# Small-block row lists loaded with the expert's other lists, and one semaphore for each small-block row buffer

## The reference, cut to what matters

```
eid_s = eid[order]; tok_s = order // TOP_K; gate_s = gates.reshape(n_asg)[order]   # sorted by expert
def expert_block(args):
    xb, e = args
    return (jax.nn.silu(xb @ w_g[e]) * (xb @ w_u[e])) @ w_d[e]
ybuf = lax.map(expert_block, (xbuf.reshape(n_blocks, MOE_BLK, D_MODEL), block_e))
y = ybuf.reshape(n_blocks * MOE_BLK, D_MODEL)[dest] * gate_s[:, None].astype(xt.dtype)
return jax.ops.segment_sum(y, tok_s, num_segments=n_tok)
```

## Time and profile before

| | us |
|---|---|
| median of three timed runs | 2811.11 |
| profiled execution, its own time | 2801.74 |
| its span (first to last instruction) | 2800.1 |
| PE busy | 2565.7 (92%) |
| DVE busy | 1757.6 (63%) |
| ACT busy | 1606.1 (57%) |
| POOL busy | 889.7 (32%) |

### The profile page before, as it was taken

One profiled execution on the slowest core, in us unless ns is written; L12 is line 12 of the kernel. 1 busy time (PEld: TensorE's weight loads), 2 busy tenths in 40 slices (PEclk: granted clock), 3 DMA queues, 4 the chain that ended last, 5 costly groups with the idle time before them and its releaser, 6 DMA issues.

```text
span 2800.1 us, 59777 instructions
## 1 busy us (share of the span) xinstructions
PE 2565.7 (92%) x19448; PEld 1802.4 (64%) x19449; DVE 1757.6 (63%) x3619; ACT 1606.1 (57%) x2613; POOL 889.7 (32%) x915
## 2 busy tenths in 40 slices
PE   5899999999999999993989899889989788889977
PEld 2345555555555555551878788778878677778866
DVE  5677777777777777776545466456646344446533
ACT  7665555555655555563646477557747445557642
POOL 1132232322322332222333344334434323324422
PEclk9899999999999999997999999999999889999988
DMA  9376666666666666667756677567767445657732
GB/s 317 73 166 164 164 153 158 157 157 154 158 164 163 154 157 157 158 149 227 226 177 181 199 257 256 160 191 255 256 203 257 149 140 164 199 187 255 251 86 46
DMA packets 551307, 507.25 MB, mean 181 GB/s; under 512 B 413803, under 2 KB 413964, under 8 KB 550236
## 3 DMA queue, kind: packets, MB, share of 16 engines
q1 hardware_dynamic: 517372, 405.56, 50.2%
q0 software_dynamic: 33744, 100.60, 14.1%
q10 hardware_dynamic: 144, 0.52, 0.0%
HBM read 322.09 MB, written 87.36 MB: 146 GB/s over the span
## 4 chain that ended last, share of the span: by engine, by line
PE 61%; DMA 21%; issue 8%; POOL 3%; DVE 3%; POOLq 2%; ACT 2%; SPq 1%; DVEq 0%; ACTq 0%
PE psG L611 11%; DMA out_rows<-y,scatter_rows 7%; PE psE L611 6%; PE psF L611 6%; PE psD L611 5%; PE psC L611 5%; PE psG L1929 5%; PE psH L1929 4%; DMA tail_more<-slot_table 4%; DMA xg_more<-hn_rows,tail_more 3%; PE psA L1891 3%; PE psB L1891 3%; PE psH L611 3%; PE psC L1891 3%; PE psD L1891 3%
## 5 line engine op out<-in xcount | busy, mean ns | idle before, releaser
L611 PE MATMUL psG<-wi_all,both_xT 128*128 128x512 f16 x1536 | 346.0, 381 | 4.4 <-DVE qsq L1402 4.4
L611 PEld LDWEIGHTS psG<-wi_all,both_xT 128*128 128x128 f16 x1536 | 148.6, 98 | 181.3 <-issue 9.9
L2022 ACT ACTIVATE unread<-wi_all 128x4096 fp8e4<-128x4096 f32 x62 | 223.7, 3607 | 0.0
L872 ACT ACTIVATE prob<-prob,soft,s_stat 128x256 f32<-128x256 f32 x256 | 150.9, 591 | 99.5 <-DVE soft L1295 99.5
L1828 POOL DMA_INDIRECT out_rows<-y,scatter_rows x79 | 166.4, 2107 | 77.0 <-POOL scatter_rows L1825 68.0
L611 PE MATMUL psE<-wo_all,both_mT 128*128 128x512 f16 x768 | 177.8, 381 | 3.0 <-DMA both_mT<-prob 2.9
L611 PE MATMUL psF<-wo_all,both_mT 128*128 128x512 f16 x768 | 176.2, 379 | 0.0
L2155 DVE SCALAR_TENSOR_TENSOR gate_lo<-wi_all,own,gate_hi 128x2048 f16<-128x2048 f32 x64 | 150.2, 2349 | 38.6 <-ACT gate_hi L2026 38.6
L611 PE MATMUL psC<-wi_all,both_xT 128*128 128x512 f16 x768 | 171.0, 379 | 0.0
L611 PE MATMUL psD<-wi_all,both_xT 128*128 128x512 f16 x768 | 171.0, 379 | 0.0
L2155 DVE SCALAR_TENSOR_TENSOR up_lo<-wi_all,own,up_hi 128x2048 f16<-128x2048 f32 x64 | 147.7, 2349 | 35.2 <-issue 33.2
(11 more groups left out here) (405 smaller groups left out, 7330.5 us busy)
## 6 DMA issues: line engine op xcount, KB each, us to landing
wi_all<-in_w_gate SPq DMA_DIRECT2D x32, 2048.0 KB
wi_all<-in_w_up SPq DMA_DIRECT2D x32, 2048.0 KB, 12.6
wi_all<-in_w_down SPq DMA_DIRECT2D x32, 2048.0 KB
um<-u_rows SPq DMA_DIRECT2D x64, 256.0 KB, 2.7
out_rows<-h SPq DMA_DIRECT2D x32, 512.0 KB, 3.0
xt<-in_x SPq DMA_DIRECT2D x31, 512.0 KB, 3.8
xres<-in_x SPq DMA_DIRECT2D x31, 512.0 KB, 4.6
hn_rows<-xres SPq DMA_DIRECT2D x31, 512.0 KB, 2.9
```

The source lines that it names most:

```text
L611: m = nc.tensor.matmul(ps, left[:, l, k, :], weights.half(r, k, n, width), start=(k == opens and j == 0), stop=(k == closes and j == 2))
L872: s.activation(prob[:, hd, :], prob[:, hd, :], ACT.Exp, bias=ntop[:, hd:hd + 1], scale=inv_s, accum_out=psum_[:, hd:hd + 1]).then_inc(p_sb ...
L2022: s_.activation(unread[:].bitcast(mybir.dt.float8e4), w, ACT.Abs, accum_out=sums(p, n), saturate=False).then_inc(summed, 1)
```

## The change

The lists of the first two small blocks of an expert are now loaded together with its other list, three experts ahead, into `tail_lists`. `big` on GpSimd makes three small copies from it (to `tail_now`, `more` and `first_rows`) and then gathers `xg_more`, issues the list loads for expert e+3, waits for TensorE's transposes of `xg_first`, and gathers the next expert's `xg_first`. The semaphore `tail_rows_in` is split into `first_in` and `more_in`. At the start GpSimd waits for the clearing before it loads any list. The counts of `pending_s` change with the number of copies. The loop over small blocks still reloads `more` and gathers again.

```
-        return 2 * e + 2 * t + 1
-    def more_of(e, t):
-        return 2 * e + t + (1 if is_last(e) else 2)
+        return 4 * e + 2 * t + 2
...
-        def load_list(e):
+        def load_lists(e):
             pool.dma_start(lists[:, bass.ds(e, 1)].rearrange("p o j w -> p (o j) w"),
                            table[bass.ds(e * CAP, BIG), :].rearrange("(j p) w -> p j w", p=P)).then_inc(listed_in, 16)
+            pool.dma_start(tail_lists[0:TAIL, bass.ds(e, 1)].rearrange("p o j w -> p (o j) w"),
+                           table[bass.ds(e * CAP + BIG, 2 * TAIL), :].rearrange("(j p) w -> p j w", p=TAIL)).then_inc(listed_in, 16)
...
-            pool.wait_ge(listed_in, 48 if isinstance(e, int) and e < 3 else 16 * (e + 1))
+            pool.wait_ge(listed_in, 96 if isinstance(e, int) and e < 3 else 32 * (e + 1))
...
+        def tail_of(e, i):
+            return tail_lists[:, bass.ds(e, 1), i].rearrange("p o w -> p (o w)")
+
+        def gather_tail(rows, listing, signal):
+
             pool.indirect_dma_start(rows[0:TAIL, :], None, hn_dram, bass.IndirectOffsetOnAxis(ap=listing[0:TAIL, 0:1], axis=0),
-                                    bounds_check=SEQ + P - 1).then_inc(tail_rows_in, 16)
+                                    bounds_check=SEQ + P - 1).then_inc(signal, 16)
...
         def big(e, p, r, t, ahead):
-            keep_list(first, listed(e, t) + 1)
-            list_tail(more, e, 1, 2 * e + t + 1)
-            gather_tail(xg_more, more, 2 * e + t + 1, None if is_zero(e) else turned(e, t) - 4)
             if ahead:
-                list_tail(first, e + 1, 0, 2 * e + t + 2)
-                gather_tail(xg_first, first, 2 * e + t + 2, turned(e, t) + 1)
+                pool.wait_ge(listed_in, 32 * E if ahead == 1 else 32 * (e + 3))
+            pool.wait_ge(first_in, 16 * (e + 1))
+            if not is_zero(e):
+                pool.wait_ge(more_in, 16 * (e + t))
+                pool.wait_ge(xT_ps, turned(e, t) - 4)
+            hold(pool, held)
+            g.tensor_copy(tail_now[:], tail_of(e, 0)).then_inc(pending_s, 1)
+            g.tensor_copy(more[:], tail_of(e, 1)).then_inc(pending_s, 1)
+            g.tensor_copy(first_rows[:], tail_of(e + 1 if ahead else e, 0)).then_inc(pending_s, 1)
+            pool.wait_ge(pending_s, listed(e, t) + 3)
+            hold(pool, held)
+            gather_tail(xg_more, more, more_in)
             if ahead > 2:
-                load_list(e + 3)
+                load_lists(e + 3)
+            if ahead:
+                pool.wait_ge(xT_ps, turned(e, t) + 1)
+                hold(pool, held)
+                gather_tail(xg_first, first_rows, first_in)
...
         mixed(pool)
+        pool.wait_ge(cleared, 5)
         for e in range(3):
-            load_list(e)
+            load_lists(e)
         for j in range(2):
             gather(0, j)
-        pool.wait_ge(cleared, 7)
...
-        def turn_tail(rows, number):
-
-            pe.wait_ge(tail_rows_in, 16 * number)
+        def turn_tail(rows, landed, number):
+
+            pe.wait_ge(landed, 16 * number)
...
-            turn_tail(xg_first, 2 * e + t + 1)
+            turn_tail(xg_first, first_in, e + 1)
...
-            turn_tail(xg_more, more_of(e, t) + 1)
+            turn_tail(xg_more, more_in, e + t + 1)
...
-            copy_y(2 * e + t, 0, listed(e, t))
+            copy_y(2 * e + t, 0, listed(e, t) + 2)
...
-        for listing in (first, more):
-            v.memset(listing[:], 0).then_inc(cleared, 1)
-        dve.wait_ge(cleared, 3)
-        for listing in (first, more):
-            v.tensor_copy(listing[:, 0:1], cst[:, C_JUNK:C_JUNK + 1]).then_inc(cleared, 1)
+        v.memset(tail_lists[:], 0).then_inc(cleared, 1)
+        dve.wait_ge(cleared, 2)
+        v.tensor_copy(tail_lists[:].rearrange("p e j w -> p (e j) w")[:, :, 0],
+                      cst[:, C_JUNK:C_JUNK + 1].to_broadcast([P, 2 * E])).then_inc(cleared, 1)
```

More of the change, by code:

```diff
@@ L1662, in experts @@
     aT_hi, aT_lo = sb("aT_hi", [P, KE, BIG], F32R), sb("aT_lo", [P, KE, BIG], F32R)
-    lists = sb("lists", [P, E, 2, 2], I32)
-    first, more, tail_now = (sb(f"tail_{w}", [P, 2], I32) for w in ("first", "more", "now"))
+    lists, tail_lists = sb("lists", [P, E, 2, 2], I32), sb("tail_lists", [P, E, 2, 2], I32)
+    first_rows, more, tail_now = sb("first_rows", [P, 2], I32), sb("tail_more", [P, 2], I32), sb("tail_now", [P, 2], I32)
     pending = sb("pending", [P, 2, 2], I32)
@@ L1696, in experts @@
     chosen, named, pending_s = sem("chosen"), sem("named"), sem("pending_s")
-    rows_in, tail_rows_in, added = sem("rows_in"), sem("tail_rows_in"), sem("added")
+    rows_in, first_in, more_in, added = sem("rows_in"), sem("first_in"), sem("more_in"), sem("added")
     xT_ps, xT_hi, xT_lo = sem("xT_ps"), sem("xT_hi"), sem("xT_lo")
@@ L1795, in gather @@
                                     bounds_check=SEQ + P - 1).then_inc(rows_in, 16)
[L1797 to L1809, removed]
-            pool.indirect_dma_start(rows[0:TAIL, :], None, hn_dram, bass.IndirectOffsetOnAxis(ap=listing[0:TAIL, 0:1], axis=0),
-                                    bounds_check=SEQ + P - 1).then_inc(tail_rows_in, 16)
[L1813 to L1817, removed]
+        def tail_of(e, i):
+            return tail_lists[:, bass.ds(e, 1), i].rearrange("p o w -> p (o w)")
+        def gather_tail(rows, listing, signal):
+            pool.indirect_dma_start(rows[0:TAIL, :], None, hn_dram, bass.IndirectOffsetOnAxis(ap=listing[0:TAIL, 0:1], axis=0),
+                                    bounds_check=SEQ + P - 1).then_inc(signal, 16)
         def scatter(d, s):
@@ L1850, in tail @@
             g.tensor_copy(pending[:, 0, :], tail_now[:]).then_inc(pending_s, 1)
-            pool.wait_ge(pending_s, listed(e, t) + 2)
+            pool.wait_ge(pending_s, listed(e, t) + 4)
             hold(pool, held)
-            keep_list(more, listed(e, t) + 3)
-            list_tail(more, e, i + 2, more_of(e, t) + 1)
-            gather_tail(xg_more, more, more_of(e, t) + 1, turned(e, t) + 2)
+            g.tensor_copy(tail_now[:], more[:]).then_inc(pending_s, 1)
+            pool.wait_ge(pending_s, listed(e, t) + 5)
+            pool.wait_ge(more_in, 16 * (e + t + 1))
+            hold(pool, held)
+            pool.dma_start(more[0:TAIL, :], table[bass.ds(e * CAP + BIG + (i + 2) * TAIL, TAIL), :]).then_inc(tail_in, 16)
+            pool.wait_ge(xT_ps, turned(e, t) + 2)
+            pool.wait_ge(tail_in, 16 * (t + 1))
+            hold(pool, held)
+            gather_tail(xg_more, more, more_in)
         def close(e, p, r, t0, t, ahead):
@@ L1869, in gpsimd @@
         mixed(pool)
+        pool.wait_ge(cleared, 5)
         for e in range(3):
-            load_list(e)
+            load_lists(e)
         for j in range(2):
             gather(0, j)
-        pool.wait_ge(cleared, 7)
         pool.dma_start(out[SEQ:SEQ + 1, 0:8], cst[0:1, 0:8]).then_inc(added, 16)
-        list_tail(first, 0, 0, 0)
-        gather_tail(xg_first, first, 0, None)
-        pend(0, 1)
+        g.tensor_copy(first_rows[:], tail_of(0, 0)).then_inc(pending_s, 1)
+        pool.wait_ge(pending_s, 1)
+        hold(pool, held)
+        gather_tail(xg_first, first_rows, first_in)
+        pend(0, 2)
         for j in range(2):
@@ L2100, in close @@
             act.wait_ge(added, emptied(2 * e + t))
-            copy_y(2 * e + t + 1, 0, listed(e, t))
+            copy_y(2 * e + t + 1, 0, listed(e, t) + 2)
         s_.preload_act_table_set("silu_and_others")
```

## The result

The changed kernel takes 2665.4 us, the median of four runs (2662.46 to 2666.88); beside them the kernel before took 2810.82 (four runs, 2808.14 to 2812.12). The ratio is 0.9482, with a 95% interval of 0.9466 to 0.9499. The forecast was 2664, its range 2654 to 2686. The profiled execution has a span of 2662.9 us and took 2664.5.

What follows compares the result with a forecast made beforehand. TensorE bounds the kernel (92% busy), with 122.4 us of waits before `xg_more`'s transposes, put down to `xg_first`. Gain 154 and start loss 7 sum to -147; 2801.7 becomes 2655, with the 9.4 offset 2664, range 2654 to 2686.

Steps and rivals of the forecast that it cites:

- Part 1: Small-block transposes on TensorE: own semaphores and earlier `xg_more` remove the wait and its slow clock, gain 154 us.
- the late bound: Landing of `xg_more` in expert 21 if held by the scatter: 2286.9, still before TensorE's need at 2287.7.
- Part 2: Behind the small block's transposes: psG's products and the scaling of y find what they need in time; no new wait.
- Part 3: GpSimd's changed list loads and added copies lie beside TensorE's work: cost nothing, 19 us if uncovered.
- the long copies that were weighed: Copies in `big` at the longest seen (2.30 and 1.77 us): `xg_more` 1.9 us late, 27 us less gain.
- Part 4: The start: lists wait for VectorE's clearing, first transposes come later; loss +7 us, from +4.3 to +9.
- The sum: All terms together: -154 + 7 = -147 us against the profiled execution.
- (a): Rival, 10%: `xg_more` lands after T+27.8, held by the scatter or slow copies; 7 to 60 us, middle 2690.
- (b): Rival, 6%: the small block's scatter 1 is slow, so TensorE gets up-weights late; 35 us, 2699.
- (c): Rival, 6%: lists bring nothing, `xg_more` is gathered as late as now; 13 to 40 us, 2690.
- the one long case: Within the rival of useless lists: one small block keeps a wait of some 5.5 us, beside 13 of 0.6.
- (d): Rival, 2%: GpSimd bounds every expert; threshold 19.6 us for three copies and waits ahead; at 22 us, 2884.

Runs made afterwards that it cites:

- delay_32: `start_early` with 32 small copies on GpSimd ahead of the three copies in `big`, in every expert; 2661.1 us, ratio 0.9478.
- sem_only: The kernel before with one semaphore for each row buffer, GpSimd's lists, gathers and order unchanged; 2666.1 us, ratio 0.9504.
- lists_only: The changed kernel with the single semaphore for both gathers back; 2686.2 us, ratio 0.9569.
- delay_64: `start_early` with 64 small copies on GpSimd ahead of the three copies in `big`, in every expert; 2915.8 us, ratio 1.0390.
- start_early: The changed kernel, but the three 256-row lists and first two gathers don't wait for the clearing; 2653.1 us, ratio 0.9450.
- weights_rows: `start_early` with expert 1's weight loads held back on SyncE until both first gathers have landed; 2656.8 us, ratio 0.9460.
- before_wait_clear: The kernel before with GpSimd's wait for the clearing moved ahead of the three list loads; 2819.7 us, ratio 1.0051.
- before_again: The kernel before, unchanged, profiled a second time; 2807.5 us, one run.

## Why the prediction was right, and where it was not

**Part 1, own semaphores and `xg_more` first: right, with one mis-sized landing.** The mechanism and the sum hold: 150.6 us against 154. The gather was put at T+19.6 and came at T+19.57. The landing was taken at T+24.6 and was T+26.6, inside the late bound (2286.9 was T+27.0). Between the two bounds, "3.82 us after its start" and "3.82 us after the scatter", the prediction took a value near the early one, and the late one was right: in expert 21 the gather is full 3.6 us behind the scatter's last recorded update (3 of its 16 are recorded), and in experts 1 to 30 it is 2.0 to 4.7 us behind it. In experts 2, 9 and 29, where all 16 are recorded, it is 3.3, 4.7 and 3.0 us. So the slack was 1.1 us where 3.2 was taken, and `delay_32` shows how near its edge is. The semaphore and the lists were forecast as one term; `sem_only` and `lists_only` show that either alone takes most of it (142 and 122 us, the second with the loss at the start), and that they overlap.

**Inside Part 1: where the 3.4 us went.** The fourteen experts with a small block behind expert 0 gained 153.1 us together, against 154. What else is missing lies in the last expert, 2.2 us, within what it varies by, and for 0.6 us in experts without a small block. The 153.1 hold one surprise: expert 1 took 3.6 us more than expert 21. TensorE stood (first row) for 1.84 us with no releaser, and had the slow clock soon after (psG's twelve products took 4.53 us):

```profile
1423.61 0.19 PE L1894 MATMUL psB<-tT_hi,up_lo 128*128 128x64 f16 x1 [1.84 <-issue]
1423.99 0.76 PE L1925 MATMUL psE<-cst,xg_more 64*128 64x64 f32 x8
```

All runs with the early lists, but for `delay_64`, took 50 to 51 us there; `sem_only`, without them, took 47.8. Before, some 1 us of it lay ahead of a wait that covered it. That the missing clock comes from this stall is read from the order of the rows; no experiment took it away, and what the stall itself is stays open.

**Part 2, nothing late next: right.** No new wait of TensorE at psG or psC, and no other engine shows in expert 21.

**Part 3, other work on GpSimd free: right.** Experts without a small block stay at 34.90 us with GpSimd at 16.40 (four of them take 0.1 to 0.2 us more). In the changed kernel the 96 copies to `tail_now`, `tail_more` and `first_rows` in `big` last 0.19 us in the median and the longest 0.28, so the long copies that were weighed did not occur there. They did at the start of `start_early` (VectorE and GpSimd, in order of time):

```profile
1341.05 4.49 DVE L2172 TENSOR_TENSOR down_lo<-wi_all,down_hi 128x2048 fp32r<-128x2048 f32 x2
...
1341.12 2.26 POOL L1833 COPY tail_more<-tail_lists 128x2 int32<-128x2 int32 x1
...
1343.31 2.26 POOL L1834 COPY first_rows<-tail_lists 128x2 int32<-128x2 int32 x1
```

Each copy ends within 0.1 us of one of VectorE's two instructions of 2.25 us. By the rule of the Trainium skill, "SBUF — State Buffer", section "Who interferes with whom", that GpSimd's reads of SBUF and a VectorE instruction with two SBUF inputs exclude one another for the whole instruction, it should be so; the trace agrees.

**Part 4, the start: right in kind, the size wrong.** Forecast +7 with 9 as the high end, measured +13.4 (0.45 of it was already there when the first part ended). The step gave 6.1 us for the later lists, 1.8 for three more of them, and left the landings as they were. The issue was right (7.0 us later). Mis-sized are the lists' landing (5.52 instead of 2.16 us) and the gather's (8.48 instead of 7.45), 4.4 us together: a delay of 7 us put both among the 2 MB loads of expert 1. For the gather `weights_rows` shows that this is the cause; for the lists `before_wait_clear` shows that the delay alone does it. The assumption that the gather might land sooner, "the weight loads are further on", had the sign wrong.

**The sum and the median.** By profiled executions the sum was -147 against -137.2 measured: 6.4 from Part 4 and 3.4 from the experts. The medians differ by -145.4. The offset of 9.4 us between before's median and its profiled execution was carried over as if it belonged to every kernel; but the changed kernel's profiled execution lies within 1 us of its median. `before_again` accounts for 5.8 us of it, nearly all in the waits before `xg_more` (122.4 against 128.0 us), which are gone; where the rest lay no run shows. So it should have been dropped for the most part, and 2655 with the right size of the start (+6.4) and of the experts (+3.4) is 2665. That the forecast of 2664 stands so near is luck.

**The rivals.** (a) came near (1.1 us of slack) and appears in `delay_32`, at 8 us. (b) did not occur. (c) named the amount left by the semaphore alone as 13 to 40 us and 2690; `sem_only` has 14.9 us of waits and two slow clocks, 13 us above `start_early`: the light end of that price, and no loss at the start, hence 2666. Its "some 5.5 in the one long case" was 1.5. (d) is real, and its threshold was too high: copies of 9.4 us and stalls of 4.4, in the mean over the 32 experts of `delay_64`, make 13.8 us, under the 19.6 worked out, and the kernel is slower than before. Its sum had neither the fetching of instructions, which no row of before showed, nor the late `xg_more` of the small blocks (54.0 instead of 46.5 us).

## What to carry to other kernels

Where a wait on a counted semaphore is put down to a transfer that the waiting instruction doesn't read, give each buffer its own semaphore first: here that alone was worth 142 us, without one operation less, where the whole change was worth 145 and the whole change without its late start 155. A step moved behind a wait is to be priced with the traffic that it will meet at its new time, not with its old landing times; 7 us of delay cost 13. And the landing of a transfer that goes out while another of the same issuer is under way is to be counted from the landing of that one: here 3.6 us behind the scatter, not 3.82 us from its own issue.

## What the hardware showed that was not expected

- A list of 1 or 2 KB landed in 2.1 to 2.3 us ahead of the weight loads and in 5.5 to 6.1 us among them; a gather of 128 rows in 4.4 to 4.7 us without them, in 7.4 to 8.6 us with them.
- A gather of 64 rows took 3.82 us with nothing of GpSimd's under way, and 7.0 us behind a scatter, 3.6 us after the last recorded update of that one's semaphore.
- GpSimd stood for 7.3 to 12.5 us in 13 of 32 experts with 64 more copies in its loop body, three instruction packets fell into each stall, and that queue moved 0.76 MB instead of 0.20. With 32 copies no such stall was seen.
- Waits of 1.5 to 1.8 us were sometimes followed by the slow clock (psG 4.48 and 4.60 us) and sometimes not (1.74 us, clock 1.00). In `lists_only` a wait of 2.38 us came twice, once with psG at 4.61 us behind it and once at 3.02.
